# Contiguous 8 KB expert weight runs, an expert gather split by sequence, and one PSUM bank moved, in a two-block fp32 transformer kernel

## What is computed

```python
mods = silu(c) @ ada_w[i] + ada_b[i]         # 6 x 1024: sh1 sc1 g1 sh2 sc2 g2; cmods from c_ctx
h2 = rms_norm_2(x_new, n2) * (1 + sc2) + sh2
x_new = x_new + g2 * expert_choice_ffn(h2, router, w_gate, w_up, w_down)

def expert_choice_ffn(h, router, w_gate, w_up, w_down):   # 16 experts, 1024 x 1024 each
    cap = 2 * t // 16                                     # 32 tokens per expert and sequence
    aff = softmax(h @ router)
    gates, idx = top_k(swapaxes(aff, 1, 2), cap)
    xs = h[idx]
    y = (silu(xs @ w_gate) * (xs @ w_up)) @ w_down * gates
    return zeros(t, d).at[idx].add(y)
```

## Time and profile before

| | |
|---|---|
| median of 3 runs | 2748.7 us (2746.15 to 2752.49) |
| the profiled execution: its own time | 2742.69 us |
| its span | 2740.9 us |
| TensorE busy | 2207.3 us (81%) |
| ScalarE, VectorE, GpSimd busy | 627.5, 759.3, 730.6 us |
| bytes moved by DMA | 635.90 MB |
| mean granted TensorE clock | 0.900 |

### The profile page before, as it was taken

The page is one execution under the profiler, slowest core; times in us unless marked ns, Lnnn a source line. Parts: engine busy times, 40 slices in busy tenths (PEclk is TensorE's granted clock), DMA queues, the critical chain, the costliest instruction groups (busy, mean ns, idle before and its releaser), DMA issues.

```text
span 2740.9 us, 30970 instructions
## 1 busy us (share of the span) xinstructions
PE 2207.3 (81%) x12020; PEld 1412.3 (52%) x12020; DVE 759.3 (28%) x1433; ACT 627.5 (23%) x896; POOL 730.6 (27%) x610
## 2 busy tenths in 40 slices
PE   7969878989788888979798899999969875555554
PEld 6848667968577677845454443343347541111111
DVE  4662220122621200148453211221146530000001
ACT  3524232333533233321241010000011410000000
POOL 6618165796253556900200000000000100000000
PEclk9979989999889899999898899999989888888887
DMA  7415567654135476641101699999963039999996
GB/s 249 137 33 184 173 227 247 208 177 140 61 123 200 169 246 215 205 168 73 62 1 61 249 409 409 410 410 410 409 236 125 21 125 409 409 409 410 410 409 253
DMA packets 220672, 635.90 MB, mean 232 GB/s; under 512 B 10041, under 2 KB 16441, under 8 KB 220425
## 3 DMA queue, kind: packets, MB, share of 16 engines
q1 hardware_dynamic: 217520, 623.79, 60.6%
q0 software_dynamic: 2880, 10.29, 1.4%
q10 hardware_dynamic: 152, 0.17, 0.0%
HBM read 633.17 MB, written 1.05 MB: 231 GB/s over the span
## 4 chain that ended last, share of the span: by engine, by line
PE 58%; DMA 18%; DVE 11%; issue 5%; SPq 4%; ACT 3%; POOL 2%; DVEq 0%; ACTq 0%
PE bank L974 11%; DMA ring<-in_w_gate 9%; PE bank L480 8%; PE bank L482 8%; PE bank L481 8%; PE bank L846 5%; DMA ring<-in_w_down 4%; SPq L1061 4%; PE bank L550 3%; DMA ring<-in_w_up 3%; PE bank L986 2%; PE bank L997 2%; PE bank L604 2%; PE bank L855 2%; POOL ring_r L1125 1%
## 5 line engine op out<-in xcount | busy, mean ns | idle before, releaser
L1125 POOL TENSOR_TENSOR ring_r<-ring,ring_r 128x512 fp32r<-128x512 f32 (+1 forms) x544 | 666.2, 1273 | 428.1 <-ACT ring_r L1210 428.0
L974 PE MATMUL bank<-ring,arena 128*64 128x512 f32 (+1 forms) x3072 | 574.3, 685 | 232.6 <-DMA ring<-in_w_gate 80.2
L480 PE MATMUL bank<-ring_r 128*128 128x256 f32 (+1 forms) x1504 | 469.6, 312 | 90.9 <-issue 46.8
L974 PEld LDWEIGHTS bank<-ring,arena 128*64 128x64 f32 (+1 forms) x3072 | 172.2, 137 | 616.9 <-issue 604.5
L1210 ACT ACTIVATE ring_r<-ring 128x2048 fp32r<-128x2048 f32 (+1 forms) x138 | 253.7, 1840 | 503.2 <-PE bank L482 227.7
L482 PE MATMUL bank<-xT_r,ring_r 128*128 128x256 f32 x1248 | 360.4, 289 | 0.0
L481 PE MATMUL bank<-ring_r 128*128 128x256 f32 x1248 | 359.2, 288 | 0.0
L480 PEld LDWEIGHTS bank<-ring_r 128*128 128x128 f32 x1504 | 295.9, 197 | 117.2 <-issue 50.3
L482 PEld LDWEIGHTS bank<-xT_r,ring_r 128*128 128x128 f32 x1248 | 246.4, 197 | 0.0
L481 PEld LDWEIGHTS bank<-ring_r 128*128 128x128 f32 x1248 | 245.0, 196 | 0.9 <-issue 0.7
L1155 POOL TENSOR_TENSOR arena<-const 128x1024 f32<-128x1024 f32 x6 | 12.5, 2081 | 796.1 <-DVEq L1628 726.9
(11 more groups left out here) (270 smaller groups left out, 2481.6 us busy)
## 6 DMA issues: line engine op xcount, KB each, us to landing
ring<-in_w_gate SPq DMA_DIRECT2D x128, 1024.0 KB, 18.1
ring<-in_w_up SPq DMA_DIRECT2D x128, 1024.0 KB, 18.4
ring<-in_w_down SPq DMA_DIRECT2D x128, 1024.0 KB, 18.4
ring<-in_ada_w SPq DMA_DIRECT2D x48, 1024.0 KB, 5.2
ring<-in_ffn_w_gu SPq DMA_DIRECT2D x40, 1024.0 KB, 5.4
ring<-in_ffn_w_down SPq DMA_DIRECT2D x20, 1024.0 KB, 5.1
ring<-in_mem_wkv SPq DMA_DIRECT2D x16, 1024.0 KB, 5.1
ring<-in_w_in SPq DMA_DIRECT2D x16, 1024.0 KB, 14.2
```

Of the source, the lines that this page charges most:

```text
L480: pe.matmul(dst, w_hi, v_hi, start=first, stop=False)
L974: mm = pe.matmul(dst[nb][W * j:W * j + W, :], src[:, 2 * q + c, W * j:W * j + W], wide_of((u0 + k) % RING)[:, c, UN * nb:UN * nb + UN], st ...
L1125: pool.tensor_tensor(lo[:, c], whole[:, c], hi_of(u)[:, c, 0:n], ALU.subtract).then_inc(*signal("w_lo", (u, c)))
```

## The change

1. Expert loads use `(p c) n -> p c n`: partition `p` gets rows `8 p` to `8 p + 7`, so that the two rows of a load are neighbours, one run of 8 KB. All rows of the contraction are permuted by this, feature `8 p + c` in the place of `128 c + p`.
2. To match it, `gather` reads the array weights from `xhat` with a step of 8 elements (32 bytes), and the transposes of `moe_h` do likewise. They now wait for both halves of `moe_h` before the first.
3. `gather` multiplies each token tile with the 64 columns of its own sequence in layer 0 (128 columns with zeros before). In layer 1 there is one sequence and the columns stay 128.
4. Gain and shift are needed in the new order of features: GpSimd spreads them (`spread`), TensorE folds them with a 0/1 matrix (`refold`: four small matmuls in layer 0, two in layer 1), VectorE copies them to `moe_mods`. Two 0/1 matrices are made once on VectorE.
5. The transposes of `ada_T` go to PSUM bank 4 and not to the rotation of banks 0 to 3.

```diff
+        row16 = sb("row16", [P, 16])
+        col8 = sb("col8", [P, KC])
+        spread = area(3072, 4, KC, 16)
+        moe_mods = gcols[:, :, :, :, :].rearrange("p a b c d -> p (a b c d)").rearrange("p (k c s) -> p k c s", k=2, c=KC)
...
             def ada_T(l, g):
                 pe.wait_ge(*after("mods_rows", (l, g)))
-                b = dense_bank(("modsT", l, g))
+                b = open_bank(("modsT", l, g), 4)
...
                 mm.then_inc(*filled_now(("posT", layer)))
+                pe.wait_ge(*after("spread", layer))
+                b = dense_bank(("refold", layer))
+                for j in range(2):
+                    for s in range(seqs):
+                        at = KC * (2 * j + s)
+                        mm = pe.matmul(b[:, at:at + KC], spread[:, 2 * j + s].rearrange("p c r -> p (c r)"), col8[:, :], start=True, stop=True)
+                mm.then_inc(*filled_now(("refold", layer)))
...
-                            for n, t in enumerate(tiles):
-                                mm = pe.matmul(bank[6 + h][:, P * c:P * c + P], xhat[:, t, P * (4 * h + c):P * (4 * h + c) + P],
-                                               moe_pick[:, t, :], start=(n == 0), stop=(n == len(tiles) - 1))
+                            for t in tiles:
+                                dst, one = (v.rearrange("p (e s k) -> p e s k", e=G, s=seqs)[:, :, t // 2, :]
+                                            for v in (bank[6 + h][:, P * c:P * c + P], moe_pick[:, t, :]))
+                                mm = pe.matmul(dst, xhat[:, t, :].rearrange("p (f c) -> p c f", c=KC)[:, 4 * h + c, :], one,
+                                               start=(t % 2 == 0), stop=(t % 2 == 1))
...
                     pe.wait_ge(m["g_sb"], i + 1)
+                    pe.wait_ge(m["hid"], 2 * i + 2)
                     for nb in range(2):
-                        pe.wait_ge(m["hid"], 2 * i + 1 + nb)
                         for q in range(4):
-                            mm = pe.transpose(bank[4 + nb][:, P * q:P * q + P], moe_h[:, 512 * nb + P * q:512 * nb + P * q + P], ident)
+                            mm = pe.transpose(bank[4 + nb][:, P * q:P * q + P], moe_h[:, :].rearrange("p (f c) -> p c f", c=KC)[:, 4 * nb + q, :], ident)
...
-                        view = w[name][layer, expert(j + (G if k >= U else 0))].rearrange("(c p) n -> p c n", p=P)
+                        view = w[name][layer, expert(j + (G if k >= U else 0))].rearrange("(p c) n -> p c n", c=KC)
...
                 gate_diag(layer, 1, seqs)
+                for j, v in enumerate((gain[:, 1], shift(layer, 1))):
+                    for s in range(seqs):
+                        ins = pool.tensor_tensor(spread[:, 2 * j + s], v[:, :, s:s + 1].to_broadcast([P, KC, 16]),
+                                                 row16[:, :].unsqueeze(1).to_broadcast([P, KC, 16]), ALU.mult)
+                ins.then_inc(*signal("spread", layer))
...
             link(dve.memset(aff[:, :, :, NE:], 0.0))
+            link(dve.tensor_reduce(row16[:, :], ident.rearrange("p (r c) -> p r c", c=KC), AX.X, ALU.add))
+            link(dve.tensor_reduce(col8[:, :], ident.rearrange("p (r c) -> p c r", c=KC), AX.X, ALU.add))
...
+                key = ("refold", layer)
+                dve.wait_ge(*full(key))
+                for j in range(2):
+                    folded = bank_of(key)[:, 2 * KC * j:2 * KC * j + KC * seqs].rearrange("p (s c) -> p c s", c=KC)
+                    ins = dve.tensor_copy(moe_mods[:, j, :, 0:seqs], folded)
+                link(ins)
+                drop(key)
...
-                            a = gain[:, 1, 4 * h:4 * h + 4, s:s + 1].unsqueeze(3).to_broadcast(shape)
-                            b = shift(layer, 1)[:, 4 * h:4 * h + 4, s:s + 1].unsqueeze(3).to_broadcast(shape)
+                            a, b = (moe_mods[:, j, 4 * h:4 * h + 4, s:s + 1].unsqueeze(3).to_broadcast(shape) for j in range(2))
```

More of the change, by code:

```diff
@@ L89 @@
           "mods_rows", "mods", "diag", "gates_bc", "u_in", "uconv", "u_norm", "yb", "xhat", "hT", "hT_odd", "aff_exp", "w_hi", "w_lo", "xT_hi", "y_hi", "y_lo", "h_full", "h_hi", "gate_w_hi",
-          "aff", "top", "out_dma", "ab_in", "logit_max", "router_in", "u_in2", "uvar", "ssq2", "short", "ssq_act", "cleared")
+          "aff", "top", "out_dma", "ab_in", "logit_max", "router_in", "u_in2", "uvar", "ssq2", "short", "ssq_act", "cleared", "spread", "refold")
 def weight_plan(w):
```

## The result

The changed kernel takes 2763.9 us (median of 5 runs, 2762.9 to 2771.1) against 2746.2 us before (5 runs, 2744.4 to 2752.5): ratio 1.0065, 95% interval 1.0048 to 1.0083. It is slower, by 17.7 us, where 2687 us were forecast. The profiled execution took 2762.9 us, its span is 2761.1 us (before 2740.9).

What follows compares the result with a forecast made beforehand. TensorE was taken to pace block 1's feed-forward part and DMA block 2's experts, TensorE close behind in layer 0. Terms -39 - 12.5 - 13.4 + 1.7 + 1.0 + 0.7 = -61.5 us gave 2681.2, plus 6.0 for the median: 2687, range 2676 to 2758.

Steps and rivals of the forecast that it cites:

- Parts 2 and 3, gather with a step of 32 bytes: Gather's array-weight loads, read at every eighth element: step priced at 0, bounded by 0 and a doubled or tripled load.
- the load just doubles: Rival on stepped weight loads: 0.107 us more on each of 608 loads, 65 us, time 2752; chance 0.20.
- the rival's "for it": Argument for the more-than-doubled load (chance 0.13): faster DMA uses up TensorE's 14 us of slack in layer 0.
- halving these to 64 gains nothing: Gather in layer 0: the 128-column weight load sets the pace, so 64 moving columns gain nothing.
- Bank 4: Block 1, L480 after the modulation transposes: four waits for a PSUM bank mostly vanish, -39 us.
- Runs of 8 KB: Expert loads of block 2: longer DMA packets save 12.5 us in layer 0 and 13.4 in layer 1.
- Refold: Small TensorE products before the first gather: +1.7 us in layer 0, +1.0 in layer 1; block 2's starting reductions +0.7.
- hidden: POOL's four small products ahead of its memsets in the refold: 1.2 us more, hidden before VectorE needs the last memset.
- Merged wait: Wait for both halves of `moe_h`: free where the 7.34 us gather precedes it, under 1 us in each layer's last group.
- Packets: Expert-stage DMA: 8 KB packets cost 310.6 ns instead of two at 160, giving about 422 GB/s.

Runs made afterwards that it cites:

- bank 4 alone: The kernel before with only the modulation transposes moved to PSUM bank 4: 2701.1 us against 2748.6, ratio 0.9829.
- the version with two copying engines: Changed kernel with 128 gather columns, plain gather reads, features reordered once per layer by VectorE and ScalarE, refold before picks: 2676.3 us against 2751.2.

## Why the prediction was wrong

**The step that failed** is "Parts 2 and 3, gather with a step of 32 bytes", where it says "I take 0". A record of the gather takes 15.44 / 64 = 0.241 us instead of 0.115: 2.1 times as long. The reason given, that the load's 202 ns against the transposes' 141 ns in the earlier trace rows leave room, does not hold: the gather's loads went from 192 to 335 ns (medians) with the step. The difference between two durations in rows of pipelined loads did not tell what fills them. The prediction called this its weakest step and had "the load just doubles" as a rival, at 0.107 us for each of 608 loads, 65 us. In fact only the 544 loads of gathers pay. At 0.126 us each they would make 68.5 us; the first gathers pay less (9.7 to 15.5 us in layer 0, 6.3 to 7.9 in layer 1, against 7.3 to 15.4 in a group). The runs give 67.6 together with the refold and the merged wait. The 64 transposes' loads pay nothing on the path: at full clock the eight of a group take 1.04 or 1.05 us (1.04 before), though their loads' median rises from 141 to 192 ns; that the matmuls' own time covers it is my reading, no run shows it. In layer 0 nothing absorbed the rest: faster DMA had left TensorE as the bound, as the rival's "for it" said.

**What no case had**: the rival gave 2752 us, 12 below the result. The sentence "halving these to 64 gains nothing" is right for the gather's time and wrong for what follows. 64 columns with the doubled load let the clock fall in each of layer 0's groups, 23.8 us in all. Why the two together do it and neither alone stays open. Against this stand the larger gains of two terms below.

**Bank 4**: forecast -39. The mechanism was right, and the size a little small: the four stretches are 42.3 us shorter, 10.6 each instead of 9.65. The spans show -42.8 and the medians -47.5 (interval of the ratio 0.9812 to 0.9845, so 43 to 52). The router's matmuls come in another phase of the clock, and the profiled execution of before is the earliest of the five with the stalls at L550; how much of the 47.5 us is either is not shown.

**Runs of 8 KB**: forecast -25.9, measured -28.6. 422 GB/s and 119.4 us a group in layer 1 are as worked out. In layer 0 the forecast's 59.6 us come only in the last groups, the others take TensorE's 58.6; the gain there is 14.0 us by the spans, 12.5 forecast. In the changed kernel layer 0 has none of it, since TensorE paces there: with the step and 128 columns the groups are 66.7 us apart with runs of 4 KB and of 8 KB alike.

**Refold**: forecast +2.7 with the reductions for both layers. In layer 0 it is lost in the spread. From L554 to the first gather the changed kernel takes 94.3 us, bank 4 alone 94.6. The products do hold GpSimd up, and VectorE's picks wait for the memset:

```profile
1468.76 1.20 POOL L1197 TENSOR_TENSOR arena<-gain,row 128x128 f32<-128x128 f32 x2
...
1471.74 3.51 POOL L1204 MEMSET xT<- 128x4096 f32 x1
...
1475.39 0.29 DVE L2198 TENSOR_TENSOR arena<-posT,const 128x128 f32<-128x128 f32 x1 [3.02 <-POOL xT L1204]
```

so "hidden" was wrong: TensorE's wait for the picks ahead of the first gather is 4.7 us, with bank 4 alone 2.0. But the same shift gave VectorE about as much back (below). In layer 1, from gather to gather, it is 0.6 to 1.2 us, with 1.0 forecast: 313.8 us without the refold, 314.5 in the version with two copying engines, 315.0 in the changed kernel with plain reads.

**Merged wait**: as forecast, under 1 us in each layer's last group. TensorE's waits name it:

```profile
PE bank L1029 <- DVE arena L2233: 3.2, 2, 1.6
```

These are two waits of 1.6 us, one a layer; before, they were of 1.0 (L1016). **Packets**: as forecast, 421 and 422 GB/s where DMA paces.

**The terms as measured**: bank 4 -47.5, runs of 8 KB -28.6, step with refold and merged wait +67.6, the 64 columns +23.8. Each is the difference between two of a chain of kernels, so that their sum, +15.3 us, is the changed kernel against the before of that session by construction and confirms nothing; the result's own pair gives +17.7, since its runs of before have a median 2.4 us lower.

## What to carry to other kernels

A layout that makes DMA's runs longer moves the reordering to somebody; price the read on the engine that repeats it most, per instruction, before counting the gain. For fp32 weights of TensorE a step of 16 or 32 bytes doubled the load (0.115 to 0.236 and 0.241 us a record); if the order must change, change it once, on an engine that is waiting anyway. And when two engines are within a few per cent of each other, a gain on one is worth little more than the slack of the other, while any cost on the other counts in full.

## What was not expected of the hardware

- The stepped load does not follow the clock. The first gather of the changed kernel, with 1.2 GHz granted until 1498.1, took 15.49 us, the later ones, which begin at 2.4 GHz, 15.44, and those with 128 columns, wholly at 2.4 GHz, 15.43. A plain gather with 64 columns took 13.9 us at the low clock and 7.29 at the high one.
- Two parts that each left the clock at 2.4 GHz in layer 0's groups let it fall to 1.2 together, which cost 23.8 us.
- One VectorE instruction on a small tile, L2144 in the kernel before, takes 5.07 us while GpSimd's memsets run. In the changed kernel, where the refold pushed these memsets later, it takes 0.69 us (L2164). The kernel with bank 4 alone, VectorE and GpSimd:

```profile
1465.87 5.06 DVE L2144 TENSOR_SCALAR arena<-arena 48x256 f32<-48x256 f32 x1
...
1467.27 3.51 POOL L1186 MEMSET xT<- 128x4096 f32 x1
```

  and the changed kernel:

```profile
1468.26 0.69 DVE L2164 TENSOR_SCALAR arena<-arena 48x256 f32<-48x256 f32 x1
```

  With bank 4 alone the instruction ends at 1470.93, just after the memset (1470.78). The Trainium skill (SBUF — State Buffer, "Who interferes with whom") says that VectorE and GpSimd share a pair of ports under an exclusive lock; the end right behind the memset agrees with it. That the memsets are the cause is read from this overlap: the instruction starts at 1465.87, before the first of three memsets (1466.35), and no run was made for it alone.
- Open: why a step costs the transposes' loads 51 ns and the gather's 143 ns (medians 141 to 192 and 192 to 335). Loads of different kinds of matmuls were not taken apart.
